# The recurrence of a two-model forward pass: score products regrouped and moved, within the order of one stage

## The chip, the cores and the metric

One core of one Trainium2 chip. The time is device microseconds of one execution.

## The reference

Two blocks run one after the other on a sequence of 512 tokens with 1024 features, each with two layers. The change touches the second block's recurrent branch only (16 heads of width 64), once in each of its two layers:

```python
def rwkv7_scan(r, w, k, v, a, b):
    def step(state, inp):
        r_t, w_t, k_t, v_t, a_t, b_t = inp
        sa = jnp.einsum('bhvk,bhk->bhv', state, a_t)
        state = (state * w_t[:, :, None, :] + sa[..., None] * b_t[:, :, None, :]
                 + v_t[..., None] * k_t[:, :, None, :])
        return state, jnp.einsum('bhvk,bhk->bhv', state, r_t)
```

Its inputs come from projections of the normalised input, each mixed with the row before it: r, k and v; a decay and a rate of low rank; `kk = k * k_k` brought to unit length per head (the key unit); a = -kk and b = kk * rate. Its output is normalised per head, gets a bonus `sum(r * k * r_k) * v`, and is multiplied by a gate.

## The kernel before, in words

Features lie on the 128 partitions, the 512 tokens along them. Every matmul with weights is three: weights and activations are split into a high and a low part. Weights stream through a ring of four pieces of 128 x 1024 (`Ring`, L98): GpSimd's queue loads the high part (L129), ScalarE writes its negative into the low part (L162), and GpSimd's queue adds the raw weights to that (L133). `ws.high(st, u)` (L198) is where ScalarE's order says that all pieces up to unit u + 1 are to be negated. A piece can be loaded when the one four places earlier is used.

`rwkv_b` (L1938) is the stage of the change. It takes two heads at a time (a pair, 8 pairs), one head on each half of the partitions, and the sequence in 8 chunks of 64. There is no planner: the order on each engine is written out by hand, one program for each of TensorE, ScalarE, VectorE and SyncE, and semaphores tie them. For one pair p:

- **Dense** (`dense`, L2094): decay and rate products (`decays`, "w" and "a"), then the projections k, r and v of 24 matmuls each, the sum of squares of the key ("ssq", bank 3), the variance of pair p-2 ("var", bank 4), the gate product "g" (L2129, L2130) and the bonus product. Single products of full width go through `whole` (L2053, recorded as L2054).
- Around it, ScalarE copies projections out of the PSUM banks (`copy_out`, L2282) into two staging buffers z; VectorE mixes each with its shifted self (`shift`, L2454); both build the scaled queries rt, the scaled unit key at_ and keys a and kt (L2499 to L2533).
- **Scores**: `scores(p, 0)` (L2144) makes the factor's transpose into bank 2, `scores_four` (L2164 straight, L2167 crossed quadrants) in three parts makes the key products (banks 5 and 2) and the factor itself (bank 3), `turned(p, 0)` (L2183) turns v, and `scores(p, 1)` (L2149) makes the query scores into bank 3 once VectorE has read that bank (`first_x`, L2554). ScalarE copies the transposed factor to mabt (L2381); VectorE masks the others (`keep_low` L2543, `keep_mrb` L2548).
- **Levels**: the inverse of a triangular matrix is built in five levels, each with `lower` (mabt times x), a ScalarE copy of it (pp), `inverse` (into bank 5) and `inverse_t` (into bank 4), each of 16 small matmuls with two records apiece (all of them recorded as L2091). VectorE writes them into x and its transpose under a mask (`add_x`, `add_xt`, recorded as L2552). `turned(p, 1)` and `turned(p, 2)` lie in the first two.
- **Chain**: the recurrence over the 8 chunks of pair p-1 takes 24 steps (L2056 to L2085), three kinds in turn: products for rhs; the product with the inverse (L2076) for uu; output and state (L2080 to L2084). VectorE copies each (L2443, L2445, L2448). These steps stand one by one between the products of pair p, in TensorE's order and in VectorE's alike; a step of TensorE waits for VectorE's copy of the one before.
- **Post** (`post`, L2461): the output of pair p-2 is normalised (ScalarE `keep_y`, `log_var`, `rstd`; VectorE L2465), gets the bonus (L2466) and the gate (L2468).

In the first pair there is no chain. After the last one the gate projections follow, with its chain between them. Banks are claimed by the table `order` (L1990): `claim` makes TensorE wait until the bank's last reader in the table is done, `read(name, p)` is that reader's signal.

In PE's order, L2227 to L2244 is the loop over the pairs:

```python
                dense(p)
                chain_on()
                scores(p, 0)
                chain_on()
                for first, last in ((0, 3), (3, 6), (6, 8)):
                    scores_four(p, first, last)
                    chain_on()
                turned(p, 0)
                chain_on()
                scores(p, 1)
                chain_on()
```

Of the kernel before, what the change touches and what calls it, by code (L numbers as in the profile page):

```python
# [1937 lines left out]
def rwkv_b(run, io, l, ws, again, nxt, y_all, y_hi, y_lo, gate):  # L1938

    with ExitStack() as ctx:  # L1940
# [50 lines left out]
        for p in range(PAIRS):  # L1991
            wide = [("w", p, 2, p_free), ("a", p, 5, p_free)]
            order += wide if p else []
            if p >= 2:
                order.append(("var", p - 2, 4, pn_free))
            order += [("k", p, 0 if p else 1, p_free)] + ([] if p else wide)
            order += [("r", p, 1 if p else 0, p_free), ("ssq", p, 3, pd_free), ("v", p, 0 if p else 1, p_free),
                      ("g", p, 1 if p else 0, p_free), ("bonus", p, 4, pd_free)]
            for j in range(3):
                order.append((f"t{j}", p, j % 2, p_free))  # L2000
# [24 lines left out]
        def gate_bank(m):  # L2025
            return banks[(2, 5, 3, 4)[m % 4]]

# [15 lines left out]
        def _(pe):  # L2043
# [49 lines left out]

            def dense(p):  # L2094
                def decays():
                    if p == 0:
                        pe.wait_ge(wa_made, 1)
                    pe.wait_ge(low_in[p % 2], 32 * (p // 2 + 1))
                    if p:
                        pe.wait_ge(f_free, 2 * p)  # L2100
                        pe.wait_ge(x_made, 5 * p)
                    whole("w", p, lr[0:64, p % 2, :], wa[0:64, :], lr_made)
                    whole("a", p, lr[64:128, p % 2, :], wa[64:128, :], lr_made)

                def variance(k):
# [5 lines left out]
                def key_norm():  # L2111
                    pe.wait_ge(sq_made, p + 1)
                    if p:
                        pe.wait_ge(cx_kept, 5 * p)
                    whole("ssq", p, bones[:, :], e0, ssq_made)

                if p:
                    decays()
                ws.project(pe, claim("k", p), hh, hl, between=variance)
                if p == 0:  # L2120
                    decays()
                ws.project(pe, claim("r", p), hh, hl)
                if p:
                    key_norm()
                ws.project(pe, claim("v", p), hh, hl, between=lambda k: key_norm() if p == 0 and k == 2 else None)
# [10 lines left out]
            def scores(p, j):  # L2136

                b = p % 2
                if j == 0:
                    pe.wait_ge(at_made, p + 1)  # L2140
                    pe.wait_ge(*read("w", p))
                    for c in range(NC):
                        for s_, o_ in crossed:
                            mm = pe.matmul(banks[2][o_, cut(c)], a[s_, cut(c)], at_[b][s_, cut(c)], start=True, stop=True)  # L2144
                else:
                    pe.wait_ge(x_made, LEVELS_ * p + 1)
                    for c in range(NC):
                        for s_ in heads:
                            mm = pe.matmul(banks[3][s_, cut(c)], a[s_, cut(c)], rt[b][s_, cut(c)], start=True, stop=True)  # L2149
                mm.then_inc(f_made, 1)  # L2150

            def scores_four(p, first, last):

                b = p % 2
                if first == 0:
                    pe.wait_ge(rt_made, p + 1)
                    pe.wait_ge(*read("ssq", p))
                    pe.wait_ge(*read("a", p))
                for c in range(first, last):
                    if c == 4:  # L2160
                        pe.wait_ge(ab_made, p + 1)
# [4 lines left out]
                    for s_, o_ in crossed:  # L2166
                        up = pe.matmul(banks[3][o_, cut(c)], at_[b][s_, cut(c)], a[s_, cut(c)], start=True, stop=True)  # L2167
# [20 lines left out]
            def lower(p, i):  # L2188
                n = LEVELS_ * p + i
                pe.wait_ge(x_made, n + 1)  # L2190
                if i:
                    pe.wait_ge(cx_kept, n)
                else:
                    pe.wait_ge(b_free, p + 1)
# [10 lines left out]
            def inverse_t(p, i):  # L2205
                pe.wait_ge(cx_kept, LEVELS_ * p + i + 1)
                pe.wait_ge(xt_made, 6 * p + i + 1)
                if i == 0:
                    pe.wait_ge(*read("bonus", p))
# [7 lines left out]
            for p in range(PAIRS):  # L2217
# [7 lines left out]
                scores(p, 0)  # L2225
# [6 lines left out]
                scores(p, 1)  # L2232
                chain_on()
                for i in range(LEVELS_):
                    lower(p, i)
                    chain_on()
                    if i < 2:
                        turned(p, i + 1)
                        chain_on()
                    if i < LEVELS_ - 1:  # L2240
                        inverse(p, i)
                    chain_on()
                    inverse_t(p, i)
                    chain_on()  # L2244
            steps = iter(range(24))
# [29 lines left out]
        def _(act):  # L2275
# [6 lines left out]
            def copy_out(name, p, f, n):  # L2282

                act.wait_ge(*ws.done(n + 1))
                if f >= 2:
                    act.wait_ge(z_free, f - 1)
                do(z[:, f % 2, 1:S + 1], bank(name, p)[:, :], ACT.Copy, signal=read(name, p))
# [9 lines left out]
            def log_var(p):  # L2297
                act.preload_act_table_set(LN_EXP)
# [36 lines left out]
            for p in range(PAIRS):  # L2335
                n, f = 3 + 3 * p, 3 + 3 * p
                if p >= 2:
                    keep_y(p - 2)
# [16 lines left out]
                if p:  # L2355
                    act.wait_ge(tr_made, 3 * p)
                act.wait_ge(z_free, f + 1)
                do(e0, ks, ACT.Square, scale=col("k_k", p), signal=(sq_made, p + 1))
                if p < 2:
                    act.preload_act_table_set(LN_EXP)  # L2360
                copy_out("r", p, f + 1, n + 1)
# [3 lines left out]
                do(e0, cum, ACT.Exp, signal=(eb_made, p + 1))  # L2365
                act.preload_act_table_set(TANH_EXP)
                ws.high(st, n + 3)
                copy_out("v", p, f + 2, n + 2)
                act.wait_ge(g_made, p + 1)
                if p >= 2:  # L2370
                    act.wait_ge(y_done, p - 1)
                do(gg[:, p % 2, :], bank("g", p)[:, :], ACT.Copy, signal=read("g", p))
# [22 lines left out]
                for i in range(LEVELS_):  # L2395
# [5 lines left out]
                    if i < 2:  # L2401
                        keep_turned(i + 1)

# [7 lines left out]
            for m in range(KD):  # L2411
# [9 lines left out]
                if m == 1:  # L2421
                    log_var(PAIRS - 2)
                    rstd(PAIRS - 2)
                if m == 6:
                    log_var(PAIRS - 1)
# [5 lines left out]
        def _(dve):  # L2431
# [21 lines left out]

            def shift(f, name, p, dst, mu):  # L2454

                dve.wait_ge(*read(name, p))
                do(dve.tensor_tensor(dst, z[:, f % 2, 0:S], z[:, f % 2, 1:S + 1], ALU.subtract))
                do(dve.scalar_tensor_tensor(out=dst, in0=dst, scalar=mu, in1=z[:, f % 2, 1:S + 1],
                                            op0=ALU.mult, op1=ALU.add), (z_free, f + 1))

            def post(p):  # L2461

                y, b = y_all[:, p, :], p % 2
                dve.wait_ge(yr_made, p + 1)
# [825 lines left out]
```

## Time and profile before

| | |
|---|---|
| median of 3 runs | 4006.92 us (4004.0 to 4008.68) |
| the profiled execution | 4011.43 us, span 4009.6 us |
| TensorE matmul busy | 3778.5 us, 94% of the span |
| weight loads (beside the matmuls) | 3042.1 us, 76% |
| VectorE busy | 2020.4 us, 50% |
| ScalarE busy | 1698.7 us, 42% |
| GpSimd busy | 800.9 us, 20% |
| granted TensorE clock, mean | 0.984 of full speed |
| HBM read | 612.89 MB, 153 GB/s over the span |

PE is TensorE's matmul side, PEld its weight loads, DVE VectorE, ACT ScalarE, POOL GpSimd. Times in rows are in microseconds from the span's start, durations of one instruction or group. Matmul ends are modelled, so neighbouring matmuls overlap in the records. A bracket at the end of a row is the idle time of the engine before it, and what ended it.

### The profile page before, as it was taken

The numbers are of one execution on the slowest core, as the hardware profiler recorded it, in microseconds if no ns is written. First come the engines' busy times: TensorE is split into PE (matmuls) and PEld (weight loads), VectorE is DVE, ScalarE is ACT, GpSimd is POOL, SyncE is SP. The second block draws the span as 40 slices with busy tenths as digits, with TensorE's granted clock in tenths as the row PEclk, the third lists the DMA queues.
The fourth block names the chain that finished last, engine by engine and source line by source line (L and its number), as shares of the span: only waits on it lengthen the run. The fifth ranks groups of instructions, "written<-read, shape, count | busy, mean of one in ns | idle before, by whom it ended". The sixth has DMA issues, their size and how long they took to land.

```text
span 4009.6 us, 68639 instructions
## 1 busy us (share of the span) xinstructions
PE 3778.5 (94%) x28412; PEld 3042.1 (76%) x28412; DVE 2020.4 (50%) x3578; ACT 1698.7 (42%) x2505; POOL 800.9 (20%) x1120
## 2 busy tenths in 40 slices
PE   7989999998999999989999999998999999999997
PEld 5777788777778877877777788876777777778885
DVE  4585651247553127356663476225645565357603
ACT  3475332346533237455553332235744544342223
POOL 1112222211222221200001222221120000222221
PEclk9999999999999999999999999999999999999998
DMA  9946998984699975733324889986583222779896
GB/s 306 232 97 141 278 243 188 234 216 106 137 208 194 192 171 114 178 86 69 69 61 98 176 189 192 193 176 143 114 183 74 54 63 53 158 172 192 191 193 139
DMA packets 191750, 628.90 MB, mean 157 GB/s; under 512 B 22992, under 2 KB 28368, under 8 KB 191056
## 3 DMA queue, kind: packets, MB, share of 16 engines
q0 software_dynamic: 160704, 549.53, 63.0%
q1 hardware_dynamic: 28176, 70.79, 5.1%
q8 instruction: 226, 3.70, 0.4%
q10 hardware_dynamic: 2560, 4.20, 0.4%
q14 instruction: 84, 0.69, 0.1%
HBM read 612.89 MB, written 2.10 MB: 153 GB/s over the span
## 4 chain that ended last, share of the span: by engine, by line
PE 51%; DVE 6%; DMA 3%; ACT 2%; issue 1%; SPq 0%; POOL 0%; DVEq 0%; ACTq 0%
PE bank L229 13%; PE bank L231 12%; PE bank L230 12%; PE bank L2091 4%; PE bank L2054 1%; DVE rw_z L2552 1%; PE bank L1772 1%; PE bank L1754 1%; PE bank L1745 1%; PE bank L2080 1%; DMA at_sw<-at_raw 1%; ACT gate L2280 1%; DMA w_lo<-in_b_wup 1%; DVE x L398 0%; PE bank L2068 0%
## 5 line engine op out<-in xcount | busy, mean ns | idle before, releaser
L229 PE MATMUL bank<-h_hi,w_hi 128*128 128x512 f32 x2608 | 1066.8, 409 | 25.8 <-DMA w_lo<-in_a_wgv 6.4
L231 PE MATMUL bank<-h_hi,w_lo 128*128 128x512 f32 x2608 | 1023.7, 393 | 0.0
L230 PE MATMUL bank<-h_lo,w_hi 128*128 128x512 f32 x2608 | 1023.1, 392 | 0.0
L162 ACT ACTIVATE w_lo<-w_hi 128x1024 fp32r<-128x1024 f32 (+2 forms) x558 | 557.6, 1003 | 1034.0 <-DMA w_hi<-in_a_wgv 292.7
L229 PEld LDWEIGHTS bank<-h_hi,w_hi 128*128 128x128 f32 x2608 | 493.8, 189 | 166.1 <-issue 52.5
L230 PEld LDWEIGHTS bank<-h_lo,w_hi 128*128 128x128 f32 x2608 | 494.1, 189 | 106.3 <-issue 11.5
L231 PEld LDWEIGHTS bank<-h_hi,w_lo 128*128 128x128 f32 x2608 | 493.4, 189 | 106.9
L2280 ACT ACTIVATE gate<-bank 128x512 f32<-128x512 f32 x96 | 57.3, 597 | 230.6 <-PE bank L2091 228.4
L1509 DVE TENSOR_SCALAR fa_conv<-fa_a_in,par_a 128x512 f32<-128x512 f32 x44 | 22.3, 507 | 228.9 <-ACT fa_a_in L1449 228.5
L229 PE MATMUL bank<-fa_y_hi,w_hi 128*128 128x512 f32 x352 | 137.1, 390 | 0.4 <-DMA w_lo<-in_a_wd 0.4
L229 PE MATMUL bank<-fb_y_hi,w_hi 128*128 128x512 f32 x352 | 137.0, 389 | 0.4 <-DMA w_lo<-in_b_wd 0.4
L231 PE MATMUL bank<-fa_y_hi,w_lo 128*128 128x512 f32 x352 | 137.0, 389 | 0.0
L230 PE MATMUL bank<-fa_y_lo,w_hi 128*128 128x512 f32 x352 | 137.0, 389 | 0.0
L230 PE MATMUL bank<-fb_y_lo,w_hi 128*128 128x512 f32 x352 | 136.9, 389 | 0.0
L231 PE MATMUL bank<-fb_y_hi,w_lo 128*128 128x512 f32 x352 | 136.9, 389 | 0.0
L2829 DVE SCALAR_TENSOR_TENSOR fb_work<-fb_work,par_b 128x512 f32<-128x512 f32 x176 | 132.3, 752 | 6.3
L129 POOL DMA_DIRECT2D w_hi<-in_b_wrkv x48 | 31.4, 654 | 467.9 <-PE bank L231 467.9
L2839 DVE COPY fb_work<-bank 128x512 f32<-128x512 f32 x16 | 11.1, 691 | 210.9 <-ACT w L320 210.9
L1551 DVE SCALAR_TENSOR_TENSOR x<-bank,mods,x 128x512 f32<-128x512 f32 x16 | 12.0, 750 | 205.3 <-PE bank L231 205.3
L2826 DVE TENSOR_TENSOR fb_work<-bank,rstd 128x512 f32<-128x512 f32 x88 | 60.9, 692 | 107.0 <-PE bank L231 106.3
L133 POOL DMA_DIRECT2D w_lo<-in_a_wgv x96 | 90.3, 951 | 110.0 <-ACT w_lo L162 101.7
L129 POOL DMA_DIRECT2D w_hi<-in_b_wup x96 | 54.9, 573 | 274.7 <-PE bank L231 255.0
(466 smaller groups left out, 7505.0 us busy)
## 6 DMA issues: line engine op xcount, KB each, us to landing
w_hi<-in_a_wgv POOLq DMA_DIRECT2D x80, 512.0 KB, 5.3
w_lo<-in_a_wgv POOLq DMA_DIRECT2D x80, 512.0 KB, 7.6
w_hi<-in_b_wup POOLq DMA_DIRECT2D x80, 512.0 KB, 5.0
w_lo<-in_b_wup POOLq DMA_DIRECT2D x80, 512.0 KB, 7.4
w_hi<-in_a_wh POOLq DMA_DIRECT2D x48, 512.0 KB, 5.6
w_lo<-in_a_wh POOLq DMA_DIRECT2D x48, 512.0 KB, 5.6
w_hi<-in_b_wrkv POOLq DMA_DIRECT2D x48, 512.0 KB, 4.3
w_lo<-in_b_wrkv POOLq DMA_DIRECT2D x48, 512.0 KB, 5.4
```

The lines of the kernel that those rows point to most:

```text
L129: pool.dma_start(self.hi[:, self.span(n)], src).then_inc(self.hi_in[n % self.FLAGS], 16)
L133: pool.dma_start(self.lo[:, self.span(n)], self.pieces[n][0], accum_op=ALU.add)\
L162: st.do(st.eng.activation(self.lo[:, s], self.hi[:, s].bitcast(F32), ACT.Copy, scale=-1.0), (self.neg_made, n + 1))
L229: pe.matmul(out, self.hi[:, a], hh[:, k0 + k, :], start=first and k == 0, stop=False)
L230: pe.matmul(out, self.hi[:, a], hl[:, k0 + k, :], start=False, stop=False)
L231: mm = pe.matmul(out, self.lo[:, a], hh[:, k0 + k, :], start=False, stop=last and k == ks - 1)
L1745: mm = pe.matmul(banks[2 + g][:, 256 * j:256 * (j + 1)], rot[rows, p % 2, ib * P:(ib + 1) * P], kpad[rows, kb, ib * P:(ib + 2) * P], start ...
L1754: mm = pe.transpose(banks[4 + i // 4][:, (i % 4) * P:(i % 4 + 1) * P], s[:, u % 3, i * P:(i + 1) * P], run.eye[:, :])
L2091: mm = pe.matmul(banks[out][s_, cut(c)], lhs[s_, cut(c)], rhs_[s_, cut(c)], start=True, stop=True)
L2280: st.do(act.activation(*args, **how), signal)
L2826: do(dve.tensor_tensor(a_in[:, b, 2:S + 2], banks[n % 6][:, :], run.rstd[:, :], ALU.mult), (a_free, n + 1))
L2829: do(dve.scalar_tensor_tensor(out=conv[:, b, :], in0=a_in[:, b, j:j + S], scalar=col(f"conv{j}", n), in1=conv[:, b, :], op0=ALU.mult, op1= ...
```

## The change

All of it is in `rwkv_b`. On TensorE: the query scores move from behind `turned(p, 0)` to the place of the first scores, go into bank 2, and are interleaved matmul by matmul with the transposed factor, which now goes into bank 4; `scores_four` makes the factor (its operands swapped) beside the key products, with the transposed and the plain factor in exchanged roles: bank 3 is now what ScalarE copies, bank 4 what VectorE masks. One chain step fewer stands ahead of the levels and one more in them. The decay products of pair p+1 go into the last level of pair p; the bonus product goes behind the third level; "ssq" goes into block 5 of the query projection, "var" into block 1 of it. On VectorE and ScalarE the order follows: norm, bonus and gate of pair p-2, the second key mask and the bonus times v go between the steps of the levels; the query is shifted after at_ is made; the gate is copied at level 2. The key's staging buffer is used for k and r of one pair, the other one for v. On ScalarE the negations (`ws.high`) of a pair come later, the last at level 2.

```diff
@@ TensorE @@
+            def decays(p):
...
+                whole("w", p, lr[0:64, p % 2, :], wa[0:64, :], lr_made)
+                whole("a", p, lr[64:128, p % 2, :], wa[64:128, :], lr_made)
...
             def dense(p):
+                def sums(k):
+                    if k == 5:
+                        pe.wait_ge(sq_made, p + 1)
...
+                        whole("ssq", p, bones[:, :], e0, ssq_made)
                     if k == 1 and p >= 2:
...
                         whole("var", p - 2, bones[:, :], yq[:, :], var_made)
...
+                ws.project(pe, claim("k", p), hh, hl)
                 if p == 0:
-                    decays()
-                ws.project(pe, claim("r", p), hh, hl)
...
+                    decays(p)
+                ws.project(pe, claim("r", p), hh, hl, between=sums)
+                ws.project(pe, claim("v", p), hh, hl)
...
-                pe.wait_ge(rk_made, p + 1)
...
-                whole("bonus", p, bones[:, :], kp, bon_made)
...
+            def scores(p):
+                b = p % 2
+                pe.wait_ge(rt_made, p + 1)
+                pe.wait_ge(*read("w", p))
...
+                for c in range(NC):
+                    for s_ in heads:
+                        low = pe.matmul(banks[2][s_, cut(c)], a[s_, cut(c)], rt[b][s_, cut(c)], start=True, stop=True)
+                    for s_, o_ in crossed:
+                        up = pe.matmul(banks[4][o_, cut(c)], at_[b][s_, cut(c)], a[s_, cut(c)], start=True, stop=True)
+                low.then_inc(f_made, 1)
+                up.then_inc(f_made, 1)
...
             def scores_four(p, first, last):
...
                     if c == 4:
-                        pe.wait_ge(ab_made, p + 1)
+                        pe.wait_ge(b_free, p + 1)
...
                     for s_, o_ in crossed:
-                        up = pe.matmul(banks[3][o_, cut(c)], at_[b][s_, cut(c)], a[s_, cut(c)], start=True, stop=True)
+                        up = pe.matmul(banks[3][o_, cut(c)], a[s_, cut(c)], at_[b][s_, cut(c)], start=True, stop=True)
...
-                scores(p, 0)
+                scores(p)
                 chain_on()
                 for first, last in ((0, 3), (3, 6), (6, 8)):
                     scores_four(p, first, last)
                     chain_on()
                 turned(p, 0)
                 chain_on()
-                scores(p, 1)
-                chain_on()
+                more = p + 1 < PAIRS
                 for i in range(LEVELS_):
                     lower(p, i)
                     chain_on()
...
+                    if i == LEVELS_ - 1 and more:
+                        decays(p + 1)
                     if i < LEVELS_ - 1:
                         inverse(p, i)
                     chain_on()
                     inverse_t(p, i)
                     chain_on()
+                    if i == 2:
+                        pe.wait_ge(rk_made, p + 1)
+                        whole("bonus", p, bones[:, :], kp, bon_made)
+                        chain_on()
@@ ScalarE @@
                 if p:
                     decays(p)
                     if p >= 2:
-                        log_var(p - 2)
-                        rstd(p - 2)
+                        keep_y(p - 2)
                     first_exps(p)
-                    ws.high(st, n + 2)
                     copy_out("k", p, f, n)
+                    square()
+                    act.preload_act_table_set(LN_EXP)
...
                 do(e0, cum, ACT.Exp, signal=(eb_made, p + 1))
+                if p:
+                    copy_out("r", p, f + 1, n + 1)
+                if p >= 2:
+                    log_var(p - 2)
+                    rstd(p - 2)
                 act.preload_act_table_set(TANH_EXP)
-                ws.high(st, n + 3)
+                ws.high(st, n + 2)
                 copy_out("v", p, f + 2, n + 2)
...
-                act.wait_ge(f_made, 3 * p + 1)
-                do(mabt, banks[2][:, :], ACT.Copy, signal=(ab_made, p + 1))
-                ws.high(st, n + 4)
+                ws.high(st, n + 3)
+                act.wait_ge(f_made, 3 * p + 3)
+                do(mabt, banks[3][:, :], ACT.Copy, signal=(ab_made, p + 1))
...
+                    if i == 2:
+                        act.wait_ge(g_made, p + 1)
...
+                        do(gg[:, p % 2, :], bank("g", p)[:, :], ACT.Copy, signal=read("g", p))
+                        ws.high(st, n + 4)
```

VectorE's order behind the query scaling, before and after (a number is a chain step of pair p-1):

```
before  rt 0 v-shift bonus 1 ends 2 first_xt 3 keep_low0 first_x 4 keep_low1 5 keep_mrb 6 7 kbar
        8 add_x0 9 add_xt0 10 11 12 add_x1 13 add_xt1 14 15 add_x2 16 add_xt2 17 18 add_x3
        19 add_xt3 20 21 22 add_xt4 23   (norm, with_bonus, gated: after the scan, in the next pair)
after   r-shift rt rk 0 keep_mrb 1 v-shift(first half) 2 v-shift(second) 3 first_x 4 keep_low0
        5 ends 6 first_xt 7 kbar 8 add_x0 9 add_xt0 10 norm 11 with_bonus 12 add_x1 13 add_xt1
        gated 14 keep_low1 15 add_x2 16 add_xt2 17 bonus 18 19 add_x3 20 add_xt3 21 22 add_xt4 23
```

## Rows read from the trace of the kernel before

**Rows 1.** Busy by stretches (us, then PE, PEld, DVE, ACT, POOL, PEclk, DMA share, GB/s)
```profile
1862.75:1916.40 53.65, 49.43 (x931) 40.38 (x927) 33.37 (x63) 26.65 (x43) 4.26 (x6) 1.00 0.29 65
3026.50:3347.40 320.90, 294.20 (x5554) 240.64 (x5553) 197.89 (x375) 157.80 (x256) 25.55 (x36) 1.00 0.29 64
```

**Rows 2.** The same view, one pair cut at its phases
```profile
1863.81:1884.73 20.92, 20.92 (x84) 15.25 (x82) 13.84 (x19) 15.53 (x22) 3.39 (x5) 1.00 0.36 81
1884.73:1894.63 9.90, 7.53 (x217) 6.46 (x217) 8.13 (x17) 4.26 (x8) 0.87 (x1) 1.00 0.77 171
1894.63:1899.12 4.49, 4.49 (x138) 4.13 (x138) 2.27 (x7) 2.11 (x5) 0.00 (x0) 1.00 0.02 5
1899.12:1904.28 5.16, 4.93 (x149) 4.51 (x150) 2.85 (x7) 2.11 (x5) 0.00 (x0) 1.00 0.02 3
1908.82:1913.37 4.55, 3.86 (x136) 3.59 (x133) 2.21 (x6) 0.60 (x1) 0.00 (x0) 1.00 0.02 4
1913.37:1917.46 4.09, 3.84 (x100) 2.87 (x96) 1.88 (x6) 1.45 (x3) 0.00 (x0) 1.00 0.01 4
```

**Rows 3.** Timeline of TensorE ahead of the levels (start, us, engine, line)
```profile
1862.75 1.13 PE L2054 MATMUL bank<-rw_wa,rw_lr 64*128 64x512 f32 x4
...
1883.78 1.02 PE L2054 MATMUL bank<-gate,rw_bones 128*128 128x512 f32 x2
...
1885.02 1.05 PE L2144 MATMUL bank<-rw_ar,gate 64*64 64x64 f32 x30
...
1892.54 0.98 PE L2149 MATMUL bank<-rw_ar,gate 64*64 64x64 f32 x27
...
1894.63 0.97 PE L2091 MATMUL bank<-rw_z,gate 64*64 64x64 f32 x26 [0.71 <-DVE rw_mrb L2548]
```

**Rows 4.** Timeline of VectorE ahead of the levels
```profile
1870.12 0.75 DVE L2465 SCALAR_TENSOR_TENSOR y_all<-y_all,par_b,acc 128x512 f32<-128x512 f32 x1 [1.75 <-ACT acc L2280]
...
1887.08 0.69 DVE L2572 TENSOR_TENSOR rw_bonus<-bank,gate 128x512 f32<-128x512 f32 x1
...
1893.80 0.69 DVE L2548 TENSOR_TENSOR rw_mrb<-bank,rw_lm 128x512 f32<-128x512 f32 x1 [0.65 <-PE bank L2149]
```

**Rows 5.** Timeline of TensorE in the levels, of level 0 and level 3
```profile
1896.70 0.98 PE L2091 MATMUL bank<-gate,rw_xt 64*64 64x64 f32 x27
...
1897.86 1.15 PE L2091 MATMUL bank<-rw_xt,gate 64*64 64x64 f32 x32
...
1908.82 0.98 PE L2091 MATMUL bank<-rw_z,gate 64*64 64x64 f32 x27
...
1910.66 0.97 PE L2091 MATMUL bank<-gate,rw_xt 64*64 64x64 f32 x26 [0.45 <-ACT gate L2280]
...
1911.64 1.10 PE L2091 MATMUL bank<-rw_xt,gate 64*64 64x64 f32 x32
1912.97 0.33 PE L2080 MATMUL bank<-rw_mrb,rw_uu 64*64 64x64 f32 x4 [0.23 <-DVE rw_uu L2445]
```

**Rows 6.** Timeline of VectorE in the levels, of level 3 and level 4
```profile
1911.92 0.73 DVE L2552 COPY_PREDICATED rw_z<-rw_im,bank 128x512 f32<-128x512 int32 x1 [1.53 <-PE bank L2091]
1912.69 0.23 DVE L2445 COPY rw_uu<-bank 128x64 f32<-128x64 f32 x1
...
1913.72 0.28 DVE L2448 SCALAR_TENSOR_TENSOR rw_state<-rw_state,rw_ec,bank 128x64 f32<-128x64 f32 x1
1914.72 0.23 DVE L2443 COPY rw_rhs<-bank 128x64 f32<-128x64 f32 x1 [0.72 <-PE bank L2069]
```

**Rows 7.** Timeline of TensorE, first pair, the key's squares
```profile
1719.87 1.13 PE L2054 MATMUL bank<-w,rw_bones 128*128 128x512 f32 x2 [0.58 <-ACT w L2280]
```

**Rows 8.** Busy by stretches, first pair
```profile
1729.00:1731.80 2.80, 1.01 (x32) 0.85 (x32) 2.66 (x5) 1.55 (x3) 0.43 (x1) 1.00 0.92 174
1731.80:1735.60 3.80, 3.79 (x42) 3.42 (x40) 2.23 (x4) 0.00 (x0) 0.00 (x0) 0.55 1.02 233
```

**Rows 9.** Chain of waits, first pair
```profile
1727.11 9.03 DMA w_hi<-in_b_wrkv
```

More of the change, by code:

```diff
@@ L1991, in rwkv_b @@
         for p in range(PAIRS):
-            wide = [("w", p, 2, p_free), ("a", p, 5, p_free)]
-            order += wide if p else []
+            low = [("w", p, 2, p_free), ("a", p, 5, p_free)]
+            order += low + [("k", p, 0, p_free)] if p else [("k", p, 0, p_free)] + low
+            order.append(("ssq", p, 3, pd_free))
             if p >= 2:
                 order.append(("var", p - 2, 4, pn_free))
[L1996 to L2000, printed above, removed]
+            order += [("r", p, 1, p_free), ("v", p, 0, p_free), ("t0", p, 0, p_free), ("t1", p, 0, p_free),
+                      ("t2", p, 0, p_free), ("g", p, 1, p_free), ("bonus", p, 1, pd_free)]
         order += [("var", PAIRS - 2, 0, pn_free), ("var", PAIRS - 1, 1, pn_free)]
@@ L2130, in dense @@
                 pe.matmul(out, g2[:, p % 2, 1, :], gd[:, 1, :], start=False, stop=True).then_inc(g_made, 1)
-                pe.wait_ge(rk_made, p + 1)
+            def scores(p):
+                b = p % 2
+                pe.wait_ge(rt_made, p + 1)
+                pe.wait_ge(*read("w", p))
                 if p:
                     pe.wait_ge(xt_made, 6 * p)
-                whole("bonus", p, bones[:, :], kp, bon_made)
[L2136 to L2150, printed above, removed]
+                if p >= 2:
+                    pe.wait_ge(*read("var", p - 2))
+                for c in range(NC):
[5 more added lines that the diff above has]
+                up.then_inc(f_made, 1)
             def scores_four(p, first, last):
@@ L2284, in copy_out @@
                 act.wait_ge(*ws.done(n + 1))
[L2285 removed]
+                if 2 <= f < 6:
                     act.wait_ge(z_free, f - 1)
[L2287 removed]
+                elif f >= 6 and f % 3 < 2:
+                    act.wait_ge(z_free, f)
+                do(z[:, staged(f), 1:S + 1], bank(name, p)[:, :], ACT.Copy, signal=read(name, p))
             def keep_y(p):
@@ L2569, in add_xt @@
                     put(xt[b], 6 + i, banks[4][:, :], (xt_made, 6 * p + i + 2))
-                dve.wait_ge(bon_made, p + 1)
-                do(dve.tensor_tensor(bonus[:, b, :], bank("bonus", p)[:, :], v, ALU.mult), read("bonus", p))
+                keep_mrb()
                 step(1)
+                dve.wait_ge(*read("v", p))
+                shift_sub(f + 2, v)
+                step(2)
+                shift_add(f + 2, v, col("mu_v", p))
+                step(3)
+                first_x()
+                step(4)
+                keep_low(0)
+                step(5)
                 do(dve.tensor_copy(ec[:, b, :], e0[:, C - 1:S:C]))
@@ L2597, in _ @@
                 add_xt(1)
-                step(14, 15)
+                if p >= 2:
+                    gated(p - 2)
+                step(14)
+                keep_low(1)
+                step(15)
                 add_x(2)
@@ L2601, in _ @@
                 add_xt(2)
-                step(17, 18)
+                step(17)
+                dve.wait_ge(bon_made, p + 1)
+                do(dve.tensor_tensor(bonus[:, b, :], bank("bonus", p)[:, :], v, ALU.mult), read("bonus", p))
+                step(18)
+                step(19)
                 add_x(3)
-                step(19)
+                step(20)
                 add_xt(3)
-                step(20, 21, 22)
+                step(21)
+                step(22)
                 add_xt(4)
```

139 lines of the change are left out of this document (65 added, 74 removed).

## The prediction

> **What bounds the kernel now.** I read first the busy time by stretches, to see where the recurrence stands in the run. One pair of heads takes 53.65 us in the first layer, and in the second layer six pairs take 320.90 us, 53.5 us each [rows 1]; TensorE is busy for 92% of either at the full clock. TensorE is thus nearly the bound, and what can go is the idle 8%, plus matmul time that lies outside the stretches with idle time. The transfers take 0.3 of the DMA engines, so weights are no limit here.
>
> Then the same view, cut at the phases of one pair, counted from the first matmul of its key product at 1863.81 [rows 2]. The dense products (20.92 us) keep TensorE full. The stretch from there to the first inverse level takes 9.90 us with TensorE busy for 7.53: 2.4 us idle. The levels take 4.49, 5.16, 4.54 (what the other rows leave of 53.65), 4.55 and 4.09; the last includes the next pair's decay products. The fourth has 3.86 us of work, so 0.7 us idle.
>
> The timeline of TensorE says what is in these stretches [rows 3]: the decay products (L2054, 1.13 us) and the bonus product (1.02 us modelled, 0.95 from its start at 1883.78 to 1884.73) stand where TensorE has no idle time. The first scores (L2144) take 30 of 32 records in 1.05 us, the second scores (L2149) come at 1892.54, and the first level waits 0.71 us more for VectorE. VectorE's timeline [rows 4] gives the chain: the mask of the second scores (L2548) at 1893.80 ends the wait, and these scores in turn had to wait for VectorE to empty the bank that they write (first_x, L2557). The bonus product times value (L2572) runs at 1887.08, ahead of the copy of the chain that TensorE needs next. So TensorE waits for VectorE's queue there, not for arithmetic.
>
> **The change, part by part.**
>
> *Query scores beside the transposed factor.* L2149's 32 records are interleaved with 32 others, straight and crossed quadrants of the array in turn. Bounds: all hidden, 0.93 us (32 records at the pace of the L2144 row), or none, 1.86. I take 1.15, as the case of straight and crossed records mixed: an inverse product with the 16 records of a chain step behind it takes 1.16 us (1896.70 to 1897.86) and one with 4 such records 0.98 (1910.66 to 1911.64) [rows 5], so 12 more records cost 0.18 us. 32 more at that pace are 0.5, and I halve this since here every record has a partner. The Trainium skill (TensorEngine Tiling (Array Packing), Restrictions and Gotchas) says that different row tiles cannot access the same PSUM bank at once, which speaks against mixing four tiles over two banks. By it the 64 records would take turns. The L2144 row disagrees already for two row tiles on one bank, at 33 ns a record; no row shows four tiles on two banks for long.
>
> *The wait of the second scores goes.* In the new order VectorE masks the query scores right after them, and the third and fourth blocks of the key products need only that. I walk the queues from the first scores, in us from the key product. Dense ends at 20.0 (20.92 less the bonus product's 0.95; the two sums, over ssq and var, only change place inside it). Scores 20.3 to 21.45; mask 21.7 to 22.4; first key block to 22.3; chain copy at 22.65; second block after it to 23.8; chain 24.1; third block 24.55; chain copy 24.7; value turned 25.2 to 26.3 (L2183's eight); a chain step of 0.4; first level at 26.75. Before it was at 30.82. The value's shift (two operations, 1.5 us) now runs between the chain's copies at no cost, because TensorE is in the key products; if TensorE overtakes it, it costs up to 1.5 us. The query is shifted after the factor is made: the scores need both, and by the walk the scaled query is done at 18.95, before dense ends at 20.0. That cover is 1.0 us.
>
> *Weights.* ScalarE negates the high parts later (the last of the three at level 2, at about 39). The third piece is then used some 23 us later. ScalarE's negation and two transfers are well inside that: cost nothing. SyncE's queue is not touched; the GpSimd queue, in which each load stands behind an earlier addition, gets its additions at 19, 22 and 40 instead of close together.
>
> *Levels.* The pace comes from rows [rows 5, 6]: inverse product 1.84 us after lower product (1908.82 to 1910.66); the update of x starts 1.26 after the inverse product (1911.92) and takes 0.73; the state update 0.7 to 0.75 after its chain step; the copy of rhs 1.35 after a product starts (1914.72, the fifth level's product at 1913.37).
> Level 0: the end of the chunk's decays and the first x-transposed now stand inside it. Product 26.75; state update to 27.35; decay end and scaled factor to 28.3; rhs copy; transposed x done at 29.3, and the inverse waits for that (before: 2.07 us after the level's start, now 2.6). Behind the inverse there is now a state update ahead of the update of x, which costs 0.4. Level 0: 5.5.
> Level 1: the norm of pair p-2 (two operations of 0.75, L2465 and L2466) stands in VectorE's queue while TensorE turns keys: 4.6, before 5.16, since a chain step less stands between.
> Level 2: the bonus product goes in after the transposed inverse: 40.7 to 41.5, a chain step of 0.4, next level at 42.2. It finds no idle time, and its 0.9 is paid in full (gate copied by ScalarE at 39.3, so no wait for that): 5.4.
> Level 3: the chain's copy (L2445) now comes before the update of x. In the row it stood between the update of x and TensorE's next step [rows 5, 6]: start 1912.69, step at 1912.97, next level at 1913.37. Now the step runs beside the update: 4.3.
> Level 4: the decay products (1.06 from start to start) fall between the lower product and the transposed inverse, where TensorE waited for some 0.5: 3.6 instead of 4.09.
> The sum: 20.0 + 6.75 + 5.5 + 4.6 + 5.4 + 4.3 + 3.6 = 50.15, against 53.65: **3.5 us less per pair**.
>
> *Pair 7* has no decay products to hide: 3.0 less. *The first pair* has no chain. Its sum over the key's squares is moved from the value product into block 5 of the query product: TensorE gets there at 1715.8, but the squares are ready at 1719.87 [rows 7], so it stands for 4 us. After a stretch with 1.01 us of work in 2.80, the granted clock fell to a mean of 0.55, so mostly the 1.2 GHz level, for some 3.8 us [rows 8]; after 4 us of idleness I expect that again, which costs 1.5 us beyond the wait. Scores then start at 1731.2 instead of 1727.1, but the second scores, its masks, and the stall on the weight transfer go: 9.03 us on the chain of waits [rows 9], of which the part that delayed the level's copy was 1.3, since negation now comes at level 2. By the same walk the first level starts 0.7 earlier and its inverse 1.3. Bonus +0.9, decays -0.75: 1.2 less. The bounds are +1.5 (the wait, no gain) and -2.6 (the clock stays).
>
> The sum: per layer 6 x 3.5 + 3.0 + 1.2 = 25.2, in two layers **50.4 us**. The profiled execution took 4011.43 us (span 4009.6), so it would be 3961.0; it lies 4.5 above the median of the runs, 4006.92, from which I forecast 3956.5.
>
> **Rivals.**
> *VectorE's queue in the levels absorbs it (slower).* The order of VectorE is fixed, and the levels get norm, bonus and gate (2.2 us), the second key mask and the bonus product (1.4), and in level 0 another 2.4, of which I charged 1.0: 5.0 us more, if nothing of it is hidden [rows 4, 6]. For it: a level needs VectorE's update of x, and TensorE is in order too, so each late copy stops both chain and level. Against: VectorE is busy for only 33.4 of 53.65 us [rows 1], and 2.2 of 4.55 in a level [rows 2]. It decides if more than 3.5 of the 5.0 is exposed. In full: pairs 2 to 6 +1.5 each, pair 7 +2.0, pair 1 -0.7 (it has no norm), first -1.2: +7.6 per layer, 4022. Chance 0.05.
> *Half of that exposed:* pairs 2 to 6 -1.0, pair 7 -0.5, pair 1 -2.1, first -1.2: -8.8 per layer, 3989. Chance 0.13.
> *The quadrants take turns:* 64 records in 1.86, 0.7 more in 16 pairs: 3968. By the tiling page's rule in the Trainium skill this is what would come. Chance 0.05.
> *The levels' queue hides all:* level 0 and 2 as before except for the bonus product's gap, 48.85 per pair, 4.8 less, pair 7 4.3, first 2.6: 35.7 per layer, 3936. Chance 0.12.
> *The scores' wait only moves* (the value's shift or the query's scaling is late by the 3.5 us saved), or the change doesn't do what it says: 4007. Chance 0.05.
> The forecast itself: 0.60, 3941 to 3972 (1 us a pair either way).
>
> A measurement of this kernel can tell 0.2%, 8 us. Faster: 0.60 + 0.13 + 0.05 + 0.12 = 0.90; within 0.2%: 0.05; slower: 0.05. The range leaves out the slower case, the unchanged one and part of either neighbour: 3934 to 3988.
>
> **What would show it.** One pair at 50.2 us from key product to key product, TensorE busy 49.4 of it as before, or 98%. The first level 26.75 us after the key product, level 0 longer than before (5.5) with a wait for the transposed x (L2552's line), level 3 at 4.3. Bonus product between levels, decay products ahead of the last transposed inverse. In the first pair a wait of 4 us inside the query product and a granted clock near 0.5 behind it. I am wrong if the first level starts after +29, if TensorE waits for the query's scaling before the scores, or if the levels sum to over 25 us where I have 23.4.

## The result, and the profile after

The changed kernel takes 3987.7 us (median of 4, 3980.2 to 3991.9) against 4007.8 beside it: 0.9948 of the time, with an interval of 0.993 to 0.9966. That is 20 us less, where I had forecast 50. The profiled execution is the fastest of the four: 3980.16 us, span 3978.4, of which 6.8 us were gained ahead of the stage of the change, where nothing differs (its first key shift starts at 1704.48 instead of 1711.25).

The busy time by stretches, one pair of the changed kernel cut as in [rows 2] (dense, up to the first level, levels 0 to 4; columns: stretch and its us, PE, PEld, DVE, ACT, POOL, granted clock, DMA share, GB/s):

```profile
2008.56:2028.61 20.05, 20.05 (x85) 14.95 (x81) 12.49 (x18) 14.01 (x20) 1.32 (x3) 1.00 0.09 27
2028.61:2035.04 6.43, 5.79 (x201) 5.10 (x201) 4.73 (x10) 2.80 (x5) 2.07 (x4) 1.00 0.92 188
2035.04:2040.57 5.53, 4.98 (x155) 4.43 (x151) 4.05 (x10) 3.34 (x9) 0.00 (x0) 1.00 0.62 168
2040.57:2045.11 4.54, 4.38 (x136) 4.00 (x137) 3.92 (x8) 2.11 (x5) 0.00 (x0) 1.00 0.02 5
2045.11:2050.70 5.59, 5.29 (x142) 4.33 (x143) 4.53 (x9) 2.14 (x3) 0.86 (x1) 1.00 0.12 15
2050.70:2055.00 4.30, 3.85 (x137) 3.67 (x135) 2.16 (x5) 0.60 (x1) 0.00 (x0) 1.00 0.60 110
2055.00:2059.13 4.13, 3.76 (x93) 2.73 (x93) 1.45 (x4) 1.67 (x3) 0.00 (x0) 1.00 0.01 4
```

I had worked out 20.0, 6.75, 5.5, 4.6, 5.4, 4.3 and 3.6. The walk through the queues holds to 0.2 us a stretch, but for the second, which is 0.3 shorter, and the last, which is 0.5 longer. This pair takes 50.57 us. But it is the best of those with a norm. The same view, with whole pairs from scan to scan (the scan is VectorE's first instruction of a pair):

```profile
1852.28:1906.61 54.33, 49.58 (x928) 40.77 (x927) 33.35 (x64) 26.68 (x44) 4.27 (x6) 0.97 0.29 64
1906.61:1958.03 51.42, 48.31 (x928) 39.34 (x927) 33.37 (x64) 26.66 (x44) 4.26 (x6) 1.00 0.30 68
3055.91:3109.95 54.04, 49.65 (x927) 40.75 (x926) 33.33 (x64) 26.66 (x44) 4.27 (x6) 0.97 0.28 64
```

Pairs 1 to 6 in order: 49.0, 51.0, 54.3, 51.4, 51.6, 50.6 in the first layer, 49.3, 54.0, 51.6, 51.4, 53.8, 51.8 in the second. Before they were 53.2, 53.7, 53.6, 53.6, 53.8, 53.7 in the first and 53.3 to 54.0 in the second. What had been even is uneven now. TensorE's timeline in the pair of 54.33 us shows why:

```profile
1874.75 0.43 PE L2158 MATMUL bank<-rw_ar,gate 64*64 64x128 f32 x4
1874.96 0.33 PE L2071 MATMUL bank<-rw_state,rw_ar 64*64 64x64 f32 x2
1877.85 0.26 PE L2072 MATMUL bank<-rw_vt,rw_mk 64*64 64x64 f32 x1 [2.57 <-issue]
...
1879.36 1.96 PE L2177 MATMUL bank<-rw_cen,gate 128*128 128x128 f32 x8
```

L2071 and L2072 belong to one chain step, with no wait on a semaphore between them, yet TensorE stands still for 2.57 us, released by "issue". In the trace of the kernel before no matmul of this stage has such a wait of over 0.15 us. Now there are seven of over 0.5 us in the first layer: 1.74 (first pair), 0.75, 2.57, 0.58, 1.27, and 0.99 and 1.02 in the last pair. In the second layer there are eight, the longest 2.59, 2.48 and 1.59. The L2177 row behind the gap is a clock matter: turning v takes 1.16 us at the full clock and 1.96 here. Busy by stretches, the gap and what is behind it:

```profile
1875.30:1877.80 2.50, 0.00 (x0) 0.00 (x0) 0.40 (x1) 0.00 (x0) 0.00 (x0) 0.97 0.88 263
1877.86:1881.24 3.38, 3.38 (x42) 3.13 (x41) 1.87 (x4) 0.60 (x1) 0.00 (x0) 0.53 1.05 254
```

The engine idles, the granted clock falls to 0.53 (near the 1.2 GHz level) for the next 3.4 us, and meanwhile the DMA engines are full. GpSimd's timeline says with what: the loads (L129) and additions (L133) of weights, four within 4 us, issued 19.3 to 22.9 us after the key product. Before, the pair's six were issued at 6.9, 8.9, 12.4, 18.5, 19.1 and 24.2 us:

```profile
1870.54 0.88 POOL L133 DMA_DIRECT2D w_lo<-in_b_wrkv  x1 [12.71 <-ACT w_lo L162]
1871.10 0.87 POOL L129 DMA_DIRECT2D w_hi<-in_b_wrkv  x1
1873.63 0.87 POOL L133 DMA_DIRECT2D w_lo<-in_b_wrkv  x1 [1.66 <-ACT w_lo L162]
1874.18 0.87 POOL L129 DMA_DIRECT2D w_hi<-in_b_wrkv  x1
```

They start right when ScalarE is done with its negations, which the change moved to 18 and 21 us. But the DMA engines were nearly as full there before. The same view of both kernels, from 20 to 30 us after the key product, the kernel before first:

```profile
1883.81:1893.81 10.00, 8.34 (x219) 6.59 (x217) 7.35 (x16) 4.92 (x9) 0.87 (x1) 1.00 0.86 180
```

```profile
1871.25:1881.25 10.00, 6.92 (x190) 6.25 (x190) 4.73 (x10) 2.58 (x4) 2.14 (x4) 0.83 0.92 209
```

Instructions come by DMA too. The page's table of queues (packets, MB, share of the DMA engines' time) shows them in packets of 16 KB. By the trace of the packets, each of the 15 gaps of over 0.5 us ends 2.2 to 2.8 us after such a packet has started:

```profile
q8 instruction: 226, 3.70, 0.4%
```

In the pair of 54.33 us it starts at 1875.59, 0.3 us after TensorE has stopped.

**Theory F:** TensorE runs through its small matmuls faster than their instructions arrive, because the fetches stand behind the bunched weight transfers. **Rival R:** TensorE simply outruns its fetch, whatever the DMA engines carry. **Rival B:** bunched transfers cost any version of this kernel the same, so the change of order is blameless and the move of the negations all of it.

### The profile page after: what moved, and what is told of

It reads as the page before. It is cut to its first block, busy times and chain, and to the rows that moved or that the text cites. A ratio compares the mean times of both kernels' runs of the same rounds, so it can differ in the third digit from the quotient of the medians.

```text
span 3978.4 us, 68653 instructions
## 1 busy us (share of the span) xinstructions
PE 3767.0 (95%) x28412; PEld 3031.5 (76%) x28412; DVE 2019.4 (51%) x3578; ACT 1699.6 (43%) x2505; POOL 800.4 (20%) x1120
## 4 chain that ended last, share of the span: by engine, by line
PE 53%; DVE 4%; DMA 2%; ACT 2%; issue 1%; SPq 0%; DVEq 0%; POOL 0%; ACTq 0%
PE bank L229 13%; PE bank L230 12%; PE bank L231 12%; PE bank L2094 5%; PE bank L2057 2%; PE bank L1772 1%; PE bank L1754 1%; PE bank L1745 1%; DMA at_sw<-at_raw 1%; ACT gate L2277 1%; PE bank L2177 1%; PE bank L2079 1%; PE bank L2083 0%; DVE rw_z L2572 0%; DMA w_lo<-in_b_wple 0%
## 5 line engine op out<-in xcount | busy, mean ns | idle before, releaser
L133 POOL DMA_DIRECT2D w_lo<-in_b_wrkv x48 | 41.8, 872 | 469.4 <-ACT w_lo L162 447.9
L129 POOL DMA_DIRECT2D w_hi<-in_a_wgv x96 | 54.6, 570 | 274.7 <-PE bank L231 247.5
L133 POOL DMA_DIRECT2D w_lo<-in_a_wgv x96 | 89.7, 945 | 98.9 <-ACT w_lo L162 89.8
```

The lines of the kernel that those rows point to most:

```text
L129: pool.dma_start(self.hi[:, self.span(n)], src).then_inc(self.hi_in[n % self.FLAGS], 16)
L133: pool.dma_start(self.lo[:, self.span(n)], self.pieces[n][0], accum_op=ALU.add)\
```

## The experiments

**Transfers cut, in the changed kernel and in the one before.** Of the k, r and v weights of pairs 1 to 7 (pieces 6 to 26 of the stage) both the loads and the additions move 128 of 1024 columns. All instructions stay, and the rest of the weights is whatever lay there, so the output is another.

```diff
-        pool.dma_start(self.hi[:, self.span(n)], src).then_inc(self.hi_in[n % self.FLAGS], 16)
+        s, raw = self.moved(n, src)
+        pool.dma_start(self.hi[:, s], raw).then_inc(self.hi_in[n % self.FLAGS], 16)
...
+    def moved(self, n, src):
+        s = self.span(n)
+        return (slice(s.start, s.start + 128), src[:, 0:128]) if n in self.thin else (s, src)
```

> The changed kernel, but for the weights of k, r and v of pairs 1 to 7 only 128 of 1024 columns are moved (so these projections use stale weights; all instructions stay). Theory F: TensorE's gaps inside groups (2.57, 1.27, 1.74 us, released by issue, 17 us with the half-clock stretches behind them) come because the fetching of its instructions stands behind the weight transfers. Then the gaps over 0.5 us are gone from pairs 1 to 7, all pairs take 50.6 us, and the time is about 15 us under the changed kernel's 3988: 3970 to 3975. Rival R: TensorE uses up its instructions faster than they can be fetched, whatever else moves; then the gaps stay and the time is 3985 to 3990.

> The kernel before with the same cut of transfers. Theory F: its TensorE waits for VectorE where the transfers are, so little is to be had: 53.6 us a pair as before, time 4005 to 4008 (the first pair's stall on the weight stream stays mostly, since it is the high part of pair 1 and now short: up to 2.6 us less). Rival R: the same. If instead this kernel too gains 10 us or more, then its transfers cost it as much as the changed one, and they aren't the reason why the change brought less.

The changed kernel falls to 3960.1 us (0.9887 of before, 0.9871 to 0.9904), more than I expected by F; the one before stays at 4004.3 (0.9995, 0.9986 to 1.0004). The busy time of two pairs of the changed kernel with cut transfers, the second in the place of the one that took 54.04:

```profile
1906.98:1957.23 50.25, 47.93 (x927) 39.14 (x926) 33.36 (x63) 26.67 (x44) 4.26 (x6) 1.00 0.08 15
3052.48:3102.62 50.14, 48.01 (x928) 39.24 (x927) 33.40 (x64) 26.65 (x44) 4.27 (x6) 1.00 0.08 14
```

and of the kernel before with cut transfers:

```profile
1917.57:1971.20 53.63, 49.26 (x928) 40.26 (x927) 33.36 (x63) 26.65 (x43) 4.25 (x6) 1.00 0.07 13
```

Rival R falls: the same instructions at the same pace, and the gaps over 1 us that are left (1.60, 1.30 and 1.59 in the two layers) are all in pair 7, beside gate weights that were not cut. All pairs with a norm take 49.9 to 50.3. Between the two kernels without the traffic lie 44 us, the forecast's 50 but for 6. By their traces pairs 1 to 6 bring 22.1 and 22.3 us in the two layers, for which I had 21.0; short are the first pair and pair 7. The weight traffic costs the changed kernel 28 us by the medians (3987.7 less 3960.1), 24 by the ratios to the kernel before beside each, and 23 by the two traces of the stage; the one before it costs 2 by its ratio, and that isn't told apart from nothing. I had put the first of these at 13 to 18.

The packets show the fetch being late. In the pair of 54.33 us the packet that ends the gap starts 24.3 us after the key product, when TensorE has issued 461 matmuls and weight loads of the pair. With the transfers cut it starts at 21.8 us, after 382 of them, and no gap follows. In the kernel before it starts as late as in the changed one, at 24.5 us, but TensorE, which had waited for VectorE, has issued only 338 by then.

**The negations moved, transfers whole.** In "early" the first two of them come one place earlier each, in "late" the first comes before the copy of k, the others at levels 2 and 3.

In both:

```diff
                     first_exps(p)
+                    ws.high(st, n + 2)
                     copy_out("k", p, f, n)
```

In "early" besides:

```diff
                 act.preload_act_table_set(TANH_EXP)
-                ws.high(st, n + 2)
+                ws.high(st, n + 3 if p else n + 2)
```

(a negation that was already made is passed over, so the later calls stay as they are), and in "late":

```diff
-                ws.high(st, n + 3)
                 act.wait_ge(f_made, 3 * p + 3)
...
-                        ws.high(st, n + 4)
+                        ws.high(st, n + 3)
+                    if i == 3:
+                        ws.high(st, n + 4)
```

> The changed kernel with ScalarE's negations one place earlier: the first before the copy of k, the second where the first was, the third still at level 2 (nothing left out). The transfers then spread from 6 to 27 us after the key product instead of four within 3.7 us. Theory F: shorter gaps, 5 to 10 us under the changed kernel: 3978 to 3983. Rival R: no difference, 3985 to 3990. If the second negation delays the value's copy, 1 us a pair more.

> The changed kernel with the first negation before the copy of k, the second at level 2 and the third at level 3, so that no transfer lies in the key products and level 0 (nothing left out). Theory F: no gap between 20 and 38 us after the key product; transfers now lie beside levels 3 and 4, where TensorE issues as fast: either the gaps move there (then 3985) or they need the bunching (then 3972 to 3978). Rival R: no difference, 3985 to 3990.

"early" takes 3982.8 us (0.9938, 0.9917 to 0.9958): inside the range that I gave for F, but no clear difference to the changed kernel. The shorter gaps that F was to bring aren't there either: the longest is 2.65 us, and its pairs still reach 55.1. Its transfers are issued 6.0, 6.6, 13.3, 19.3, 19.8 and 41.5 us after the key product. So ahead of the levels they lie about where the kernel before had them, with one addition less, and the loss is there all the same. "late" (issued at 6.0, 6.6, 13.3, 40.2, 40.8 and 45.1) takes 3963.3 (0.9907, 0.9876 to 0.9937; one of its ten runs took 4018.6 at a granted clock of 0.916 and widens this). That is as good as cut transfers, with all the weights moved, and lower than both cases that I had set down for it. One of its pairs:

```profile
1909.65:1959.86 50.21, 47.89 (x927) 39.12 (x926) 33.38 (x63) 26.53 (x44) 4.28 (x6) 1.00 0.31 69
```

The share of DMA is 0.31, near that of [rows 1]; only its place is another. Four of its twelve pairs still take 50.7 to 51.7. So the amount of traffic is not what hurts, but that it lies where TensorE goes over from 85 matmuls in 20 us to 201 in 6.4. The number of matmuls alone does not explain it: the levels, where "late" has its transfers, have 137 in 4.30 us. Why they bear them better no run shows.

**The kernel before, with the change's place of the negations.**

```diff
-                    ws.high(st, n + 2)
                     copy_out("k", p, f, n)
...
                 act.preload_act_table_set(TANH_EXP)
-                ws.high(st, n + 3)
+                ws.high(st, n + 2)
...
+                ws.high(st, n + 3)
                 act.wait_ge(f_made, 3 * p + 1)
                 do(mabt, banks[2][:, :], ACT.Copy, signal=(ab_made, p + 1))
-                ws.high(st, n + 4)
...
                     if i < 2:
                         keep_turned(i + 1)
+                    if i == 2:
+                        ws.high(st, n + 4)
```

> The kernel before with only the change's move of the negations (nothing left out). It tells whether the bunched transfers alone cost time. Theory F: TensorE's idle time ahead of the levels covers most of the late instructions: 4002 to 4012, the first pair perhaps 2.6 shorter. Rival B: bunching costs any kernel the same 20 us: 4020 to 4030.

4005.8 us (0.9992, 0.9982 to 1.0003). Its pairs take 53.3 to 54.5, on the average 0.2 more than before, and its first pair about 1 us less. Rival B falls too: the bunched transfers cost this kernel next to nothing. And by "early" the loss does not need the bunch. It takes full DMA engines from some 20 us after the key product on, as the kernel before has them too, and a TensorE without idle time ahead of the levels.

**Terms of the sum, with cut transfers.** Without gaps a term can be read to some 0.1 us, from scan to scan. Each of these three was executed once (3978.6, 3970.1 and 3950.8 us), and what lies outside the stage differs by several us between executions (from the last scan to the end 654.5 to 661.0), so the pairs count here and not the times.

In "thin_sep" the crossed products come behind the straight ones of all chunks, in a loop of their own:

```diff
                         low = pe.matmul(banks[2][s_, cut(c)], a[s_, cut(c)], rt[b][s_, cut(c)], start=True, stop=True)
+                for c in range(NC):
                     for s_, o_ in crossed:
```

In "thin_dec" the decay products stand at the start of the pair's own dense part again:

```diff
-                    if i == LEVELS_ - 1 and more:
-                        decays(p + 1)
...
+                if p:
+                    decays(p)
                 ws.project(pe, claim("k", p), hh, hl)
```

In "thin_bonus" the bonus product is moved from level 2 to level 3, behind the lower product, and VectorE takes it one step later:

```diff
-                    if i == 2:
-                        pe.wait_ge(rk_made, p + 1)
-                        whole("bonus", p, bones[:, :], kp, bon_made)
-                        chain_on()
...
                     lower(p, i)
                     chain_on()
+                    if i == 3:
+                        pe.wait_ge(rk_made, p + 1)
+                        whole("bonus", p, bones[:, :], kp, bon_made)
+                        chain_on()
```

> The changed kernel with the cut transfers of 'thin_after' (k, r and v of pairs 1 to 7 move 128 of 1024 columns), so that a pair is 49.9 to 50.2 us, and with the query scores first and the transposed factor behind them instead of interleaved. If the quadrants overlap, the separate products take 0.8 to 0.9 us more and a pair takes 50.8 to 51.0; if they take turns anyhow, 50.0 as it is.

> The changed kernel with the cut transfers, and the decay products of a pair back at its start instead of in the last level of the pair before. By my sum (0.5 us of 1.06 hidden) a pair takes 50.5 instead of 50.0; if nothing was hidden, 50.0; if all was, 51.1. The last pair has none to move.

> The changed kernel with the cut transfers, and the bonus product not behind level 2 but inside level 3, between a chain step and the inverse, where TensorE waits 0.45 us for ScalarE's copy; the chain step that stood behind the bonus product moves with it. If level 2 paid the product in full, as I forecast, half of it is hidden now and a pair takes 49.5 instead of 50.0; if VectorE's queue sets the pace of these levels, 50.0 or more.

VectorE's timeline, two scans of "thin_sep", which end and start a pair of 50.58 us:

```profile
1962.03 1.23 DVE L2530 TENSOR_TENSOR_SCAN gate<-gate 128x512 f32<-128x512 f32 x1
...
2012.61 1.23 DVE L2530 TENSOR_TENSOR_SCAN gate<-gate 128x512 f32<-128x512 f32 x1
```

of "thin_dec", 50.34 us:

```profile
1962.94 1.23 DVE L2529 TENSOR_TENSOR_SCAN gate<-gate 128x512 f32<-128x512 f32 x1 [1.71 <-ACT gate L2283]
...
2013.28 1.23 DVE L2529 TENSOR_TENSOR_SCAN gate<-gate 128x512 f32<-128x512 f32 x1 [1.72 <-ACT gate L2283]
```

and of "thin_bonus", 49.47 us:

```profile
1949.24 1.22 DVE L2529 TENSOR_TENSOR_SCAN gate<-gate 128x512 f32<-128x512 f32 x1
...
1998.71 1.22 DVE L2529 TENSOR_TENSOR_SCAN gate<-gate 128x512 f32<-128x512 f32 x1
```

The pair at the same place in "thin_after" takes 49.89 (1957.23 to 2007.12). So interleaving is worth 0.7 us, the move of the decay products 0.45, and the bonus product can hide 0.4 of its time in level 3. The means over the ten pairs with a norm (50.05 in "thin_after"; 50.66, 50.48 and 49.62) give 0.6, 0.4 and 0.4. All three are within 0.2 of what was expected.

**The first pair, and the best version.** "late_p0" is "late" with the key's sum of squares later in the first pair, among the products of v at k = 2 instead of among those of r at k = 5; "late_p0_bonus" has the bonus product in level 3 too; "after_rep" is the changed kernel as it is.

```diff
-                    if k == 5:
+                    if k == (5 if p else 2):
...
-                ws.project(pe, claim("r", p), hh, hl, between=sums)
-                ws.project(pe, claim("v", p), hh, hl)
+                ws.project(pe, claim("r", p), hh, hl, between=sums if p else None)
+                ws.project(pe, claim("v", p), hh, hl, between=None if p else sums)
```

> The kernel of 'late' (3963.3, no transfers beside the key products), and in the first pair of a stage the key's sum of squares stands in block 2 of the value product, where it was before, instead of in block 5 of the query product (nothing left out). Theory: the 3.96 us of waiting and the half clock behind it go (0.63 and 0.70 granted in 5 us), the query is copied and the logarithm comes earlier by 1.3 us; the first pair is 1 to 2 us shorter in each layer: 3960 to 3962. Rival: the first pair hangs on ScalarE and VectorE, so nothing changes: 3963.

> The kernel of 'late_p0' with the same move of the bonus product, nothing left out. With half of the product hidden in 14 to 16 pairs 7 us less than 3956: 3949 to 3952. Otherwise 3956.

> The changed kernel again, on the chip of the two above: 3980 to 3992 as before.

In the changed kernel's first pair TensorE waits where I had said, and the clock falls where I had said; its timeline and then the busy time behind it:

```profile
1713.08 1.40 PE L2057 MATMUL bank<-w,rw_bones 128*128 128x512 f32 x2 [3.96 <-ACT w L2277]
```

```profile
1713.00:1718.00 5.00, 4.92 (x13) 3.43 (x14) 0.69 (x1) 2.14 (x4) 0.00 (x0) 0.66 0.00 0
```

In "late_p0" it waits 0.58 us there, at the full clock:

```profile
1718.95 1.12 PE L2057 MATMUL bank<-w,rw_bones 128*128 128x512 f32 x2 [0.58 <-ACT w L2277]
```

Most of the wait has moved, though, to the scores, where VectorE's scaling is late:

```profile
1727.63 0.37 PE L2141 MATMUL bank<-rw_ar,gate 64*64 64x64 f32 x2 [2.40 <-DVE rw_ar L2554]
```

Its first pairs take 42.7 and 42.3 us from scan to scan, those of "late" 45.8 and 44.3, so 5.1 us less in the two layers. In the whole it takes 3956.1 us (0.9865, 0.985 to 0.9879), some us under the 3960 to 3962 that I expected, and with the bonus product in level 3 3950.5 (0.9862, 0.9847 to 0.9876), beside 3983.4 (0.9949, 0.9932 to 0.9965) of the changed kernel on the same chip: 56 us under the kernel before and 33 under the changed one. That the bonus move brings something over "late_p0" rests on the pairs with cut transfers (49.5 for 49.9); the two ratios alone don't tell them apart.

## Why the prediction was wrong

The direction was right, and so were the mechanism and the size of a pair where no transfer disturbs it. The sum was wrong mainly by a term that I had set at nothing, the weights, and by some 2 us a layer in the first pair. Point by point:

- *What bounds the kernel now.* Right: idle time ahead of the levels, behind VectorE's queue.
- *The scores and their wait.* First level at 26.75 after the key product: 26.48 (20.05 + 6.43). The interleaved scores took 0.95 us (1925.91 to 1926.86 in another pair), so the lower bound of 0.93 was the right value, not my 1.15. The Trainium skill's rule against two row tiles on one bank (TensorEngine Tiling (Array Packing), Restrictions and Gotchas) is not borne out in time: 64 records went through four quadrants and two banks at 15 ns a record, and "thin_sep" shows them 0.6 to 0.7 us slower when not mixed.
- *Weights: "cost nothing".* **This step failed.** I had asked whether the weights come in time for their use, and they do. I had not asked what else uses the DMA engines at that moment. I had taken the mean share of 0.3 of a pair for "no limit", while [rows 2] shows 0.77 in the 9.90 us ahead of the levels, and this is the stretch in which I closed TensorE's waits. TensorE's own instructions come by the same engines, and its idle time had covered their lateness: cut transfers change the kernel before by nothing that can be told, and the changed one by 23 to 28 us. The move of the negations that I had described as "instead of close together" (before, the additions came at 9, 18.5 and 24 us; now it is 19, 22 and 40 to 44, with a load behind each of the first two) fills this stretch a little more, but "early" takes most of that back and gains nothing clear.
- *Levels 0 to 4.* 23.4 forecast, 24.1 measured in the pair shown, of which 0.4 is a gap by issue in level 4.
- *Pair 7.* From its key product to the first gate product it takes 51.4 and 52.0 us in the two layers, 52.6 before. That is 1.2 and 0.6 less, not 3.0. In "late" it takes 49.5 in both, which is my 3.0: what was missing here is the same failed step.
- *The first pair.* The wait was right and the clock near it, the gain of 1.2 was not. From its scan to the key product of pair 1 it takes 44.9 us in the first layer and 43.5 in the second, before 44.2 and 42.6, so 0.7 and 0.9 more. (From scan to scan it looks the same, 45.9 in both kernels, because the next pair's scan comes earlier after its key product.) In the first layer 1.74 us went to a gap by issue in the first lower product; without it my walk holds. In the second layer the kernel before had no half clock to lose, since the granted clock stayed full behind the same wait of 1.82 us, and I had taken the first layer's rows for both.
- *Rivals.* VectorE's queue did not absorb it: the pairs of 50 us with cut transfers say so. "Half of that exposed" gives 3989, close to the median measured, and is wrong all the same, since its mechanism would show in those pairs too. That its number fits is luck. Of the range, 3934 to 3988, the median is just inside its upper end.

## What to carry to other kernels

A transfer is not free just because its data come in time: ask which stretch it lies beside, and whether that stretch is one of many short instructions, whose own fetches use the same DMA engines. A mean share of the DMA engines over a loop does not answer this; the share of the stretch does. Idle time that a change takes away can have been cover for late instructions. So when a change closes waits, look at the transfers that lie beside them, also those that it leaves alone, and try them elsewhere; here a move by one place brought nothing clear, and a move behind the key products brought nearly all of it. Even pairs that turn uneven, with waits "by issue" in the middle of a group, are the sign in the profile.

## What the runs showed of the hardware

- A TensorE that runs small matmuls (201 in 6.4 us) stops for up to 2.6 us in the middle of a group while weight transfers hold the DMA engines at 0.88 to 1.05 of their time; with the transfers cut to an eighth, three gaps over 1 us are left in two layers, all beside transfers that were not cut. The stops of over 0.5 us end 2.2 to 2.8 us after a 16 KB packet of instructions has started, and with the transfers cut that packet starts some 2.5 us earlier in the pair (21.8 us after the key product for 24.3). That TensorE waits for just the instructions of this packet is inferred from this; no view shows the fetch itself waiting.
- Behind a gap of 2.57 us the granted clock fell to 0.53 for the next 3.4 us, behind one of 3.96 to 0.66 in the next 5; behind a wait of 0.58 it stayed full. A gap does not settle it by its length: behind one of 2.50 in "after_rep" and one of 2.40 in "late_p0_bonus" the clock stayed full, and behind the same wait of 1.82 us in the kernel before it fell to 0.66 in the first layer and stayed full in the second.
- Matmuls of 64x64 spread over four quadrants and two banks were issued every 15 ns, those over two quadrants and one bank every 33 ns.
